# A hybrid SSD / HGRN2 / MoE layer: the opening regrouped, from the modulation to the first convolutions

## The reference, cut to what matters

```python
mod_l = (jax.nn.silu(c) @ w_ada[layer] + b_ada[layer])[:, None, :]
mod_c = (jax.nn.silu(c_ctx) @ w_ada[layer] + b_ada[layer])[None, None, :]
sh1_l, sc1_l, gt1_l, sh2_l, sc2_l, gt2_l = jnp.split(mod_l, 6, axis=-1)
...
hl = rms_norm(xl, g_pre_mix[layer]) * (1.0 + sc1_l) + sh1_l
hc = rms_norm(xc, g_pre_mix[layer]) * (1.0 + sc1_c) + sh1_c
...
xbc_l = jax.nn.silu(dwconv_centred(xbc_l, conv_w, conv_b))
...
d = jax.nn.softplus(u.reshape(b_, t_, N_DIRS, SSM_HEADS).astype(f32) + dt_bias.astype(f32))
...
a_cs = jnp.cumsum(adt, axis=-1)
```

## Time and profile before

| | |
|---|---|
| median of 3 runs | 1957.99 us (1957.73 to 1959.09) |
| profiled execution | 1958.03 us, span of its instructions 1956.2 us |
| mean granted TensorE clock | 0.962 of full |
| busy: PE, DVE, ACT, POOL | 90%, 37%, 23%, 20% of the span |
| chain that ended last | PE 78%, DMA 14%, DVE 4% |
| PE idle ahead of its work at line 756 | 9.9 us |

### The profile page before, as it was taken

One profiled execution on the slowest core, in us unless ns is written; L12 is line 12 of the kernel. 1 busy time (PEld: TensorE's weight loads), 2 busy tenths in 40 slices (PEclk: granted clock), 3 DMA queues, 4 the chain that ended last, 5 costly groups with the idle time before them and its releaser, 6 DMA issues.

```text
span 1956.2 us, 18753 instructions
## 1 busy us (share of the span) xinstructions
PE 1770.1 (90%) x7066; PEld 955.7 (49%) x7066; DVE 718.1 (37%) x1142; ACT 448.2 (23%) x715; POOL 393.3 (20%) x473
## 2 busy tenths in 40 slices
PE   6889999999999999999999999999659788998872
PEld 1545555555647777677775444444423232443320
DVE  1534546456357555655656312213320000000004
ACT  2132241513324443434442100001200000010001
POOL 0104223142327333344433000000010000010000
PEclk9999999999999999999999999999769998999986
DMA  7203221312321111111130832504479999999993
GB/s 287 75 20 104 89 82 45 129 54 75 91 71 33 44 44 43 53 33 43 45 105 26 308 129 98 192 0 143 168 305 430 429 430 429 429 412 430 430 408 145
DMA packets 152695, 337.74 MB, mean 173 GB/s; under 512 B 13969, under 2 KB 104298, under 8 KB 140346
## 3 DMA queue, kind: packets, MB, share of 16 engines
q1 hardware_dynamic: 135098, 312.75, 41.9%
q10 hardware_dynamic: 12496, 15.75, 2.5%
q0 software_dynamic: 5040, 8.40, 1.1%
HBM read 333.51 MB, written 13.32 MB: 177 GB/s over the span
## 4 chain that ended last, share of the span: by engine, by line
PE 78%; DMA 14%; DVE 4%; issue 3%; ACT 1%; SPq 0%; POOL 0%; POOLq 0%; DVEq 0%; ACTq 0%
PE bank L756 12%; PE bank L508 11%; PE bank L2294 7%; PE bank L794 6%; DMA arena<-in_w_gate_dram 5%; PE bank L1735 5%; PE bank L513 4%; PE bank L1328 4%; DMA arena<-in_w_up_dram 3%; PE bank L2312 3%; DMA arena<-in_w_down_dram 3%; PE bank L1754 3%; PE bank L504 3%; PE bank L1737 3%; PE bank L1362 3%
## 5 line engine op out<-in xcount | busy, mean ns | idle before, releaser
L756 PE MATMUL bank<-stay,arena 128*128 128x512 f32 (+1 forms) x704 | 243.1, 501 | 9.9 <-DVE arena L1004 7.7
L2294 PE MATMUL bank<-arena 128*64 128x512 f32 x832 | 193.8, 623 | 31.2 <-DMA arena<-in_w_up_dram 15.2
L756 PEld LDWEIGHTS bank<-stay,arena 128*128 128x128 f32 x704 | 133.7, 192 | 111.7 <-issue 101.6
L508 PE MATMUL bank<-arena 128*128 128x512 f32 x384 | 168.9, 592 | 0.0
L2294 PEld LDWEIGHTS bank<-arena 128*64 128x64 f32 x832 | 67.3, 143 | 155.1 <-issue 133.0
L1232 POOL TENSOR_TENSOR arena<-arena 128x256 f32<-128x256 f32 x112 | 88.0, 786 | 267.9 <-DVE arena L1485 153.7
L2382 DVE TENSOR_TENSOR arena<-arena,bank 128x512 f32<-128x512 f32 x17 | 11.7, 688 | 296.3 <-PE bank L2294 296.3
L794 PE MATMUL bank<-arena,stay 128*128 128x512 f32 x256 | 114.6, 595 | 3.9 <-DVE arena L1043 3.9
L508 PEld LDWEIGHTS bank<-arena 128*128 128x128 f32 x384 | 71.7, 190 | 83.7 <-issue 83.7
L2191 POOL DMA_INDIRECT y_dram<-arena x17 | 17.2, 1010 | 415.5 <-DVE arena L2389 415.0
L2312 PE MATMUL bank<-arena 128*64 128x512 f32 x384 | 86.7, 604 | 14.2 <-ACT arena L2232 5.9
(11 more groups left out here) (393 smaller groups left out, 2676.0 us busy)
## 6 DMA issues: line engine op xcount, KB each, us to landing
arena<-in_w_gate_dram SPq DMA_DIRECT2D x24, 2048.0 KB, 26.1
arena<-in_w_up_dram SPq DMA_DIRECT2D x24, 2048.0 KB, 26.4
arena<-in_w_down_dram SPq DMA_DIRECT2D x24, 2048.0 KB, 26.0
arena<-in_w_in_dram SPq DMA_DIRECT2D x58, 512.0 KB, 3.8
arena<-in_w_ada_dram SPq DMA_DIRECT2D x12, 2048.0 KB, 9.9
stay<-in_w_down_dram SPq DMA_DIRECT2D x8, 2048.0 KB, 27.7
stay<-in_w_gate_dram SPq DMA_DIRECT2D x8, 2048.0 KB, 21.0
stay<-in_w_up_dram SPq DMA_DIRECT2D x8, 2048.0 KB, 24.9
```

What stands on the lines that cost most here:

```text
L508: mm = pe.matmul(b[:, :], w[:, k, :], src[:, k, 0:LAT], start=(k == 0), stop=(k == KT - 1))
L756: mm = pe.matmul(ps[:, 0:n], w[:, k, :], hT[:, k, o:o + n], start=(k == 0), stop=(k == KT - 1))
L2294: mm = pe.matmul(b[cols, :], xgT[r][:, k, cols], w[u][:, k, :], start=(k == 0), stop=(k == KT - 1))
```

## The change

In words. **Loads:** the nine row loads and the three small vectors are issued from ScalarE's queue (`load_rows`), c and c_ctx first; SP begins with x and the context, then w_ada in four slices of two k tiles by all 2048 columns, then w_dt, then w_x. **Modulation:** the stationary operand `vecs` has 32 columns a k tile, of which 30 are zero. For each k tile four matmuls follow each other, one for each 512 columns, each on its own quarter of TensorE's columns (`tile_position`) and into its own 32 partitions of bank 1. The result is copied once (128 x 512) and turned by four full transposes. All eight turn_x come between slices 1 and 2, with three banks for each kind, and are copied out unmodulated; VectorE and ScalarE modulate hT in place afterwards. A table set with both logarithm and exponential is loaded ahead of the squares. **Step sizes:** the projection starts tile by tile as hT is modulated, into banks 4 and 5. Tile 0 is projected without waiting for `DT_ABS`, tile 2 ahead of the transposes of the sums, tiles 3 and 4 behind the broadcast of the ends. Centre copies and convolutions of tiles 0 and 1 stand inside the chain.

```diff
@@ modulate_sync, load_rows
...
             sp.dma_start(xin[:, 0:LCH, :], ...).then_inc(s_x, 16)
             sp.dma_start(xin[:, LCH:NCH, :], ...).then_inc(s_ctx, 16)
             for n in range(4):
-                sp.dma_start(wada[n], w_ada_t[:, :, n * 512:(n + 1) * 512]).then_inc(s_ada[n], 16)
...
+                sp.dma_start(wada[:, 2 * n:2 * n + 2, :], w_ada_t[:, 2 * n:2 * n + 2, 0:2 * D]).then_inc(s_ada[n], 16)
+            sp.dma_start(wdt, w_in_t[:, :, OFF_DT:OFF_DT + 64]).then_inc(s_wdt, 16)
+        def load_rows(act):
+            act.dma_start(rows1[R_C:R_C + 8, :], row_tiles(c[0])).then_inc(s_rows, 16)
...
+            act.dma_start(rows2[72:96, :], row_tiles(conv_b[0])).then_inc(s_rows, 16)
...
@@ modulate_scalar
+            load_rows(act)
             act.wait_ge(s_cols, 1)
-            act.activation(sc_in[:, :], cols1[:, R_C:R_C + 16], ACT.Silu).then_inc(s_silu_c, 1)
+            act.activation(sc_in[:, :], cols1[:, R_C:R_C + 16], ACT.Silu)
+            act.wait_ge(s_zero, 1)
+            act.activation(vecs[:, :, 0:2], ..., ACT.Silu).then_inc(s_silu_c, 1)
+            act.preload_act_table_set(LOG_EXP)
...
+            for k in range(KT):
+                act.wait_ge(s_xt, 2 * k + 2)
+                act.copy(hT[:, k, LAT:T], bank[5 + k % 3][:, 0:CTX]).then_inc(s_hc, 1)
             act.wait_ge(s_mod, 1)
             for k in range(KT):
-                act.wait_ge(s_xt, 2 * k + 2)
-                act.activation(hT[:, k, LAT:T], bank[5 + k % 2][:, 0:CTX], ACT.Identity,
+                act.wait_ge(s_hc, k + 1)
+                act.activation(hT[:, k, LAT:T], hT[:, k, LAT:T], ACT.Identity,
@@ modulate_tensor
+            def ada(i):
+                pe.wait_ge(s_ada[i], 16)
+                for k in range(2 * i, 2 * i + 2):
+                    for n in range(4):
+                        mm = pe.matmul(bank[1][32 * n:32 * n + 32, :], vecs[:, k, :], wada[:, k, n * 512:(n + 1) * 512],
+                                       start=(k == 0), stop=(k == KT - 1), tile_position=(0, 32 * n))
...
             pe.wait_ge(s_xn, NCH)
-            turn_x(0)
-            turn_x(1)
+            for k in range(KT):
+                turn_x(k)
             ada(2)
-            ada(3)
-            pe.wait_ge(s_modr, 4)
-            for f in range(16):
-                mm = pe.transpose(bank[1][:, 2 * f:2 * f + 2], adar[:, f * P:(f + 1) * P], ident[0:2, 0:2])
+            ada(3).then_inc(s_ada_used, 1)
+            pe.wait_ge(s_modr, 2)
+            pe.wait_ge(s_hl, KT)
+            for q in range(4):
+                mm = pe.transpose(bank[2][:, q * P:(q + 1) * P], adar[:, q * P:(q + 1) * P], ident[:, :])
@@ modulate_vector
+            for k in range(KT):
+                dve.wait_ge(s_xt, 2 * k + 1)
+                dve.tensor_copy(hT[:, k, 0:LAT], bank[2 + k % 3][:, :]).then_inc(s_hl, 1)
+            dve.wait_ge(s_ada_used, 1)
+            dve.tensor_copy(adar[:, 0:512], bank[1][:, :]).then_inc(s_modr, 1)
...
             for k in range(KT):
-                dve.wait_ge(s_xt, 2 * k + 1)
-                dve.tensor_scalar(hT[:, k, 0:LAT], bank[3 + k % 2][:, :], amod[:, k, 0:1], modT[:, k, 0:1],
+                dve.wait_ge(s_hl, k + 1)
+                dve.tensor_scalar(hT[:, k, 0:LAT], hT[:, k, 0:LAT], amod[:, k, 0:1], modT[:, k, 0:1],
@@ ssd_scalar
             act.activation(acsT[0:64, :], dtv[0:64, :], ACT.Ln).then_inc(s_dta, 1)
+            for j in range(2):
+                for part in range(2):
+                    centre(0, j, part, True)
             act.wait_ge(s_dtt, SUMS_TURNED)
@@ ssd_tensor
-            pe.wait_ge(s_hl, KT)
-            pe.wait_ge(s_hc, KT)
             for k in range(KT):
-                pe.matmul(bank[0][0:64, :], ...)
+                pe.wait_ge(s_hl, KT + k + 1)
+                pe.matmul(bank[4][0:64, :], ...)
...
+            project(0, 0, True)
             pe.wait_ge(s_dtv, DT_ABS)
-            project(0, 0, True)
             project(0, 1, True)
+            project(0, 2, True)
             pe.wait_ge(s_dtv, SUMS)
...
+            for j in range(3, 5):
+                project(0, j, True)
             pe.wait_ge(s_dta, DECAY_EXPS - 1)
             pe.wait_ge(s_dtv, DECAY_DIFFS)
@@ ssd_vector
             own.link(dve.reciprocal(dtv[R, :], dtv[R, :]))
+            convolve(0, 0, 0, True)
+            convolve(0, 0, 1, True)
...
+            convolve(0, 1, 0, True)
+            convolve(0, 1, 1, True)
             dve.wait_ge(s_dta, DECAY_EXPS - 1)
```

More of the change, by code:

```diff
@@ L157, in build @@
         junk = take(D)
-        wada = [take(KT, 512) for _ in range(4)][::-1]
-        adar = ysT[0:2, 0:4, :].rearrange("v n f -> v (n f)")
+        wada = take(KT, 2048)
+        adar = ysT[:, 0, :]
         rows1 = take(P)
         rows2 = take(P)
-        at[0] = 24064
+        vecs = take(KT, 32)
         wdt = take(KT, 64)
+        at[0] = 24576
         dtx = take(T)
@@ L223, in build @@
         s_modr = sem("modulation_rows_copied")
+        s_zero = s_modr
         s_modst = sem("modulation_rows_stored")
@@ L398, in modulate_vector @@
                 dve.tensor_scalar(xin[:, i, :], xin[:, i, :], rst[:, i:i + 1], None, ALU.mult).then_inc(s_xn, 1)
-            for n in range(4):
-                dve.wait_ge(s_ada_used, n + 1)
-                dve.tensor_copy(adar[:, n * 512:(n + 1) * 512], bank[ADA_BANK[n]][0:2, :]).then_inc(s_modr, 1)
-            dve.wait_ge(s_turned, 2)
-            own.link(dve.tensor_tensor(modT[:, 0:16, :], bank[1][:, 0:32].rearrange("p (f v) -> p f v", v=2),
-                                       cols1[:, 0:16].unsqueeze(2).broadcast_to([P, 16, 2]), ALU.add))
+            for k in range(KT):
[3 more added lines that the diff above has]
+            dve.tensor_copy(adar[:, 0:512], bank[1][:, :]).then_inc(s_modr, 1)
+            dve.wait_ge(s_turned, 2)
+            mods = bank[2][:, :].rearrange("p (q n r) -> p n q r", q=4, n=4)
+            for v in range(2):
+                own.mark(dve.tensor_tensor(modT[:, 0:16, v].rearrange("p (n q) -> p n q", q=4), mods[:, :, :, v],
+                                           cols1[:, 0:16].rearrange("p (n q) -> p n q", q=4), ALU.add))
+            own.wait()
             own.link(dve.tensor_scalar(amod[:, :, :], modT[:, 8:16, :], 1.0, None, ALU.add))
@@ L589, in ssd_scalar, with centre @@
         def ssd_scalar(act, own):
+            def centre(g, j, s, first):
+                act.wait_ge(s_xp, START + segment(g, j, s))
+                c, (o, n, ps) = column_of(g, j), segments(j, first)[s]
+                act.activation(tile_of(j)[:, o:o + n], ps[:, 0:n], ACT.Identity, scale=cols2[:, 1, c:c + 1]).then_inc(s_xc, 1)
             act.wait_ge(s_vec, 48)
@@ L718, in group @@
                     y_tiles(g, range(4))
-            for j in range(6):
+            for j in range(2, 6):
                 for part in range(2 if j < 5 else 1):
                     centre(0, j, part, True)
-                if j:
-                    silu(0, j - 1)
+                if j == 2:
+                    silu(0, 0)
+                silu(0, j - 1)
             bc_weights(act, 1)
@@ L921, in group @@
                     head_unit(pe, 1, 2)
-            for j in range(2, 6):
-                project(0, j, True)
+            project(0, 5, True)
             turn_x(0, range(4))
@@ L956, in ssd_vector, with convolve @@
         def ssd_vector(dve, own):
+            def convolve(g, j, s, first):
+                dve.wait_ge(s_xc, segment(g, j, s))
+                v, c, (o, n, ps) = tile_of(j), column_of(g, j), segments(j, first)[s]
+                own.link(dve.scalar_tensor_tensor(v[:, o + 1:o + n], ps[:, 0:n - 1], cols2[:, 0, c:c + 1],
+                                                  v[:, o + 1:o + n], ALU.mult, ALU.add))
+                dve.scalar_tensor_tensor(v[:, o:o + n - 1], ps[:, 1:n], cols2[:, 2, c:c + 1],
+                                         v[:, o:o + n - 1], ALU.mult, ALU.add).then_inc(s_cv, 1)
             R = slice(0, 64)
```

73 lines of the change are left out of this document (26 added, 47 removed).

## The result

The changed kernel took **1923.5 us** (median of 4 runs, 1920.95 to 1925.13) against 1958.5 for the kernel before (4 runs, 1957.73 to 1963.29): 0.981 of its time, interval 0.980 to 0.983. The profiled execution took 1924.1 us with a span of 1922.5, which is 33.7 us shorter than the span of the earlier trace rows.

What follows compares the result with a forecast made beforehand. Until 144.49 us the prediction took TensorE pieces with gaps as the bound. It summed 16.9 us from the opening and 13.5 behind the step-size projection to 30.4 us less than 1958.0: 1927.6 us, range 1921 to 1942.

Steps and rivals of the forecast that it cites:

- rival E: Whole kernel: the shift does not carry, since a later stage starts on something else; no change; chance 0.02.
- rival A: Matmuls with w_ada: all four quarters at once, 1.7 us a slice; 35.8 us less, 1922.2 us; chance 0.20.
- T: End of the step-size projection: 70.9 us before, forecast 54.0; then 60.1 us to the first turn of x chunks.
- (a): Loads: all land 3.4 us earlier, x at 8.3, w_ada's slices at 16.1, 21.2, 26.4 and 31.5 us.
- (b): ScalarE and VectorE in the opening: rows' silu at about 7.8 us, squares from 9.1, x ready at about 20.8.
- rival C: Opening: the small row loads land late beside full engines; 23.3 us less, 1934.7 us; chance 0.08.
- (c): First two w_ada slices: n matmuls take n + 1 steps of 0.43 us, ending at 21.5 and 25.4 us.
- (e): Third and fourth w_ada slices: 17 steps, 7.3 us, ending at 38.6 us.
- (f): Making the modulation: 2.9 us against 3.4 before; the other products at 0.4 us each, under cover.
- (g): Step-size projection: 10.5 us, plus 2.0 us for the slow clock behind a pause.
- B: Matmuls with w_ada: no overlap in float32; 17.9 us less, 1940.1 us; chance 0.26.
- D: Opening: TensorE stays at 1.2 GHz and nothing overlaps; 13.3 us more, 1971.3 us; chance 0.03.

Runs made afterwards that it cites:

- squares first: Changed kernel with ScalarE's squares, logarithm and exponential of x ahead of the silu of c: 1924.2 us, 0.982 of the kernel before.
- opening alone: Changed kernel with its new opening kept and the step-size order of the kernel before put back: 1934.0 us, 0.987 of the kernel before.
- same quarter adjacent: Changed kernel with both k tiles of one column quarter next to each other in each slice: 1920.4 us, 0.980 of the kernel before.
- rows on SP: Changed kernel with all twelve small loads back on SP's queue ahead of x: 1925.5 us, 0.984 of the kernel before.
- both longer chains: Changed kernel with three more reciprocals in VectorE's step-size chain, written over used memory or to unread memory: 1931.8 and 1933.2 us, both 0.987.

## Why the prediction was right, and where it was not

**Direction and size: right.** Faster was given 0.95. The parts add up, and the shift at the first turn reaches the end, as the prediction had it: 1812.1 us behind it against 1811.7. Over all profiles that rest runs from 1807.7 to 1814.1 us, so "one for one" is shown to a few microseconds and not to tenths, which leaves nothing of rival E. The size owes something to the way it was made: no row could tell full overlap from none, and the forecast took the middle of the two. What came was the one end, rival A's, and the range held because it was wide enough for both.

**T to the first turn: right.** 60.1 forecast, 60.45 measured, with no wait in it. The sums were ready at T + 22.4, as worked out. The convolution of tile 2 ended at 88.01 + 0.48 = 88.49, T + 38.5; forecast at most T + 40.3. Tile 3 ended at 82.73 + 10.32, T + 43.1, so that cover was 4.6 us and not 2.6.

**(a) and (b), the loads: off by 1 to 5 us.** The first slice's matmuls started at 17.66 where its landing was put at 16.1: it gained 2 us on the 19.50 of before and not 3.4. The last slice landed at 32.5 to 33.2 us in the three runs that waited for it with SP's queue unchanged, where 31.5 was forecast, and that one sets the floor of the opening. The nine rows took until 11.05, about 5 us late: the last of them was issued at 4.70 and waited 6.3 us beside full engines. That is rival C's mechanism; its price did not come, since C let that load take 13.6 us, with x ready at 32.5. It was ready at 25.7, when the second slice was just ending (25.98). The run with the squares first settles it: x 4.6 us earlier moved nothing.

**(c) and (e), the step that failed.** "Records start in program order", hence n + 1 steps for n matmuls. A slice is 16 records on four quarters, and it took four steps: 3.64 us at 1.2 GHz, 1.92 us at full clock, where the forecast had 3.9 at full clock. The third and fourth slice took 3.61 us against 7.3, and with it the slices ended at 34.99, not 38.6: 3.6 of the 4.0 us that T was earlier than forecast. This is rival A's mechanism. The argument held against A, that two records of one matmul stand side by side in the order, weighed nothing: with even more neighbours on one quarter the time stayed, and with all on one quarter it was 3.8 times as long. What the Trainium skill says (TensorEngine Tiling (Array Packing), Key Properties), that different tiles load and multiply in parallel, is what the trace shows here in float32. The other rule (TensorE: Matmul & The Clock Gate, Part 3), by which weight loads overlap only where the row group differs, does not hold here: all four quarters share their rows, and 32 records with their loads took 3.61 us, which is eight steps of 0.43 with 0.2 left over. The same part says that matmuls start strictly in program order; the run with neighbours on one quarter speaks against that as well.

**A itself, 1922.2, was nearer than the forecast.** It had the slices end at 33.2 and T at 48.6; measured were 34.99 and 49.98. What it lacked is the landing and the length of the last slice: with x early its matmuls still ended at 34.9 (32.92 + 1.92), not at 31.5 + 1.7 = 33.2.

**(f) and (g), two errors that cancel.** "The other products run at 0.4 us, under cover, GpSimd's copies too": they ran at over 1 us each beside those copies, and the projection of the latent part took 8.67 us (37.86 to 46.53) where 7.05 were counted, 1.6 more. The 2.0 us for a slow clock behind the pause did not come in this execution. It came in another, where it cost 1.7 (8.72 for 7.05). The whole stretch from the first matmul of the projection to T took 12.1 us against 12.5. The number was right, its parts were not.

**B, D.** Both rest on matmuls that do not overlap, and fall with the 3.8. B's own sum was too low as well: the kernel on one quarter, which is B's case, had T at 70.34 and not at 66.5, 1.5 us of it from the later landing and 2.5 from the longer pause.

## What to carry to other kernels

Small matmuls with a narrow output are worth spreading over the column quarters of TensorE (both orders tried here did equally well), as far as the loads that feed them keep up; behind that point the next microsecond is in the order of the loads, not in the matmuls. A pause of TensorE is priced by what the clock does behind it too: read the granted clock of the stretch that follows, in more than one execution, before an edit that only shortens another engine's work is called a gain. And where an edit moves an early place by a few microseconds, measure that place, since the total of a long kernel scatters by as much.

## What the runs showed of the hardware

- Four float32 matmuls of 128 x 512 on the four column quarters run at once: 3.61 us for 32 records against 13.86 us on one quarter. Program order within a slice made no difference (3.67 us).
- VectorE's in-place products of 128 x 512 took 0.47 us each without GpSimd's copies (3.74 / 8) and over 1 us beside GpSimd's copies of the same size (8.24 / 8). The Trainium skill (SBUF — State Buffer, SBUF: two separate sides) calls the port pair that the two engines share an exclusive lock, for a VectorE instruction in a two-port mode or with two SBUF inputs: the one that comes second is blocked for the whole instruction. That these products are of that kind no run here shows, but a product that takes about as long as a copy (9.54 / 8 = 1.19 us) agrees with it.
- Small loads on ScalarE's queue, issued beside full DMA engines, took 6.3 us for the last of nine; ahead of the large loads, on SP's queue, the rows were turned 5.5 us earlier.
- The same pause of 2.9 us on TensorE (idle 0.8, four transposes, idle 1.4) kept the granted clock at 1.00 in seven profiles (the changed kernel, opening alone, same quarter adjacent, rows on SP, both longer chains, squares first) and lost it for 3.4 us in one. Why is open: the edit of that run changed nothing on TensorE ahead of the pause. Idle waits of 2.99 and 2.98 us for a slice, without work inside, lost it both times.
